# Two packed projections of the compression branch, each given its own duplicated weight piece

## The reference, cut to what matters

```python
(nq, nkc, nvc, nks, nvs, nkw, nvw, ngate, cq, ckv, kr, fq, fk, fv, ff) = jnp.split(h @ w_in, split_points, axis=-1)
tok_idx = jnp.arange(n_cmp)[:, None] * D_CMP + jnp.arange(L_CMP)[None, :]     # 15 windows of 32 tokens
def compress(kv, pe, w1, w2):
    blocks = kv[:, tok_idx] + pe[None, None, :, None, :]
    flat = blocks.transpose(0, 1, 3, 2, 4).reshape(B, n_cmp, G, L_CMP * DH)   # G = 2 groups, DH = 64
    return jax.nn.gelu(flat @ w1) @ w2
kc = compress(k_cmp, cmp_pe[0], cmp_w1[0], cmp_w2[0])
vc = compress(v_cmp, cmp_pe[1], cmp_w1[1], cmp_w2[1])
...
gates = jax.nn.sigmoid(h @ w_gate).reshape(B, S, 3, D_MODEL)
```

## Time and profile before

| | |
|---|---|
| median of 3 runs | 1681.83 us (1680.05 to 1681.88) |
| the profiled execution's own time | 1681.88 us |
| its span in the trace | 1680.1 us |
| PE busy | 1645.6 us, 98% |
| PEld (weight loads) busy | 1507.6 us, 90% |
| DVE, ACT, POOL busy | 62%, 43%, 32% |
| chain that ended last | PE 82%, DVE 11%, ACT 4% |
| granted TensorE clock | 0.998 of full speed |

### The profile page before, as it was taken

One profiled execution on the slowest core, in us unless ns is written; L12 is line 12 of the kernel. 1 busy time (PEld: TensorE's weight loads), 2 busy tenths in 40 slices (PEclk: granted clock), 3 DMA queues, 4 the chain that ended last, 5 costly groups with the idle time before them and its releaser, 6 DMA issues.

```text
span 1680.1 us, 34114 instructions
## 1 busy us (share of the span) xinstructions
PE 1645.6 (98%) x15064; PEld 1507.6 (90%) x15064; DVE 1033.9 (62%) x1661; ACT 714.2 (43%) x1124; POOL 539.6 (32%) x434
## 2 busy tenths in 40 slices
PE   9999999999999999999999999999999999999997
PEld 8888987899989889988888899999999899999996
DVE  5275376877774554776777877753346768643357
ACT  4444444544455544445444445432222555322223
POOL 0644613000307636321001304625542009154530
PEclk9999999999999999999999999999999999999999
DMA  9422355776546323456775544533223445332323
GB/s 353 155 101 76 129 213 204 262 280 256 184 161 234 127 76 118 155 217 243 283 281 196 176 169 146 189 107 121 102 102 130 151 149 204 111 125 101 127 77 113
DMA packets 44004, 281.46 MB, mean 168 GB/s; under 512 B 5144, under 2 KB 5272, under 8 KB 14416
## 3 DMA queue, kind: packets, MB, share of 16 engines
q1 hardware_dynamic: 42192, 270.13, 45.0%
q0 software_dynamic: 1664, 9.15, 1.4%
HBM read 278.20 MB, written 1.06 MB: 166 GB/s over the span
## 4 chain that ended last, share of the span: by engine, by line
PE 82%; DVE 11%; ACT 4%; issue 2%; DMA 0%; POOL 0%; POOLq 0%; SPq 0%; ACTq 0%; DVEq 0%
PE ps L537 79%; PE ps L545 3%; DVE part0l L1333 2%; DVE part1l L1333 2%; ACT part0h L2356 1%; ACT Xh L2356 1%; DVE rows L1757 1%; ACT part1h L2356 1%; DVE Xl L1348 1%; DVE Pr L1754 1%; ACT gates L2353 0%; DMA ring<-in_w 0%; DVE small L1364 0%; DVE sg L2020 0%; DVE x L1357 0%
## 5 line engine op out<-in xcount | busy, mean ns | idle before, releaser
L2356 ACT ACTIVATE part1h<-ring 128x1024 fp32r<-128x1024 f32 (+1 forms) x216 | 215.7, 1046 | 257.1 <-PE ps L537 245.6
L2356 ACT ACTIVATE part0h<-ring 128x1024 fp32r<-128x1024 f32 (+1 forms) x216 | 213.0, 1034 | 251.5 <-PE ps L537 241.6
L537 PE MATMUL ps<-Xh,part1h 128*128 128x256 f32 x1032 | 299.8, 291 | 6.7 <-DVE part1l L1333 2.5
L537 PE MATMUL ps<-Xh,part0h 128*128 128x256 f32 (+1 forms) x1016 | 294.4, 290 | 3.2 <-DVE Xl L1348 1.3
L537 PE MATMUL ps<-Xl,part1h 128*128 128x256 f32 x1032 | 292.6, 283 | 0.0
L537 PE MATMUL ps<-Xh,part1l 128*128 128x256 f32 x1032 | 292.3, 283 | 0.0
L537 PE MATMUL ps<-Xl,part0h 128*128 128x256 f32 (+1 forms) x1016 | 287.2, 283 | 0.0
L537 PE MATMUL ps<-Xh,part0l 128*128 128x256 f32 (+1 forms) x1016 | 287.0, 282 | 0.0
L1333 DVE TENSOR_TENSOR part1l<-ring,part1h 128x1024 fp32r<-128x1024 f32 (+1 forms) x148 | 187.9, 1309 | 58.1 <-ACT part1h L2356 57.7
L2858 POOL TENSOR_TENSOR part0l<-ring,part0h 128x512 fp32r<-128x512 f32 x136 | 173.5, 1309 | 154.8 <-ACT part0h L2356 154.8
L1333 DVE TENSOR_TENSOR part0l<-ring,part0h 128x1024 fp32r<-128x1024 f32 (+2 forms) x148 | 183.2, 1278 | 62.2 <-ACT part0h L2356 62.0
(11 more groups left out here) (413 smaller groups left out, 3275.6 us busy)
## 6 DMA issues: line engine op xcount, KB each, us to landing
ring<-in_w SPq DMA_DIRECT2D x211, 1024.0 KB, 4.9
hid<-in_ada SPq DMA_DIRECT2D x36, 512.0 KB, 5.8
hid<-in_w SPq DMA_DIRECT2D x6, 1024.0 KB, 10.7
rows<-in_lnrow POOLq DMA_DIRECT2D x6, 1024.0 KB, 9.6
fqk<-in_ada SPq DMA_DIRECT2D x6, 512.0 KB, 5.8
cq<-in_ada SPq DMA_DIRECT2D x6, 512.0 KB, 6.0
gates<-in_c SPq DMA_DIRECT2D x2, 1536.0 KB, 9.8
ring<-in_w SPq DMA_DIRECT2D x4, 512.0 KB, 5.8
```

The source lines that it names most:

```text
L537: return e.matmul(o, a, b, start=st, stop=sp)
L2356: return e.activation(o, a, ACT.Copy)
```

## The change

The piece `cmp` is replaced by two pieces, `cmpk` and `cmpv`, each a full 1 MB. Each holds its 128 columns twice: group 0, group 0, group 1, group 1, of 64 columns each. Half 0 of the new piece gives group 0 on both halves of the partitions, half 1 group 1. Both go through `gemm_half`, and `cmp_proj` becomes two copies for the keys and two for the values, each over both groups and within its own partitions. In the fills the four new halves take the slots n0 to n3; every gate half moves two places on, and the phase "m" takes ten halves in place of eight.

```diff
-FIRST = """misc fq fk fv cq0 cq1 nq0 nq1 kskw vsvw cmp g0_0 g0_1 g0_2 g0_3 g1_0 g1_1 g1_2
+FIRST = """misc fq fk fv cq0 cq1 nq0 nq1 kskw vsvw cmpk cmpv g0_0 g0_1 g0_2 g0_3 g1_0 g1_1 g1_2
...
-             "n": "cmp.0 mla0|cmp.1 mla1|g0_0.0 key1|g0_0.1 latents h0|g0_1.0 a0|g0_1.1 up h1|g0_2.0 a1|g0_2.1 turn kc|cs0 g0_3.0|cT0 g0_3.1|"
-                  "cs1 g1_0.0|cT1 g1_0.1|cv0 g1_1.0|cv1 g1_1.1|g1_2.0|g1_2.1|g1_3.0|g1_3.1",
-             "m": "g2_0.0 g2_0.1|g2_1.0 g2_1.1 OT0|g2_2.0 OT1|g2_2.1|OT3 g2_3.0|g2_3.1"}
+             "n": "cmpk.0 mla0|cmpk.1 mla1|cmpv.0 key1|cmpv.1 latents h0|g0_0.0 a0|g0_0.1 up h1|g0_1.0 a1|g0_1.1 turn kc|cs0 g0_2.0|cT0 g0_2.1|"
+                  "cs1 g0_3.0|cT1 g0_3.1|cv0 g1_0.0|cv1 g1_0.1|g1_1.0|g1_1.1|g1_2.0|g1_2.1",
+             "m": "g1_3.0 g1_3.1|g2_0.0 g2_0.1 OT0|g2_1.0 g2_1.1 OT1|g2_2.0 g2_2.1|OT3 g2_3.0|g2_3.1"}
...
-        elif name[0:4] == "cmp.":
-            m = int(name[4])
-            gemmT(l, ("cmpk", "cmpv")[m], "cmp", X, xkey(l), widths=(128,), col0=128 * m, frees=m == 1)
...
     def cmp_proj(l, s_):
-        t = bank(("cmpk", "cmpv")[s_], l)
+        b = v(bank(("cmpk", "cmpv")[s_], l)[:, :], g=2, n=256)
...
-        for g in range(2):
-            h = slice(64 * g, 64 * g + 64)
-            e.tensor_copy(M.dup[0:64, s_, g, :], t[h, 0:256]).then_inc(*V())
-            e.tensor_copy(M.dup[64:128, s_, g, 0:255], t[h, 1:256]).then_inc(*V("dup", s_, l))
+        e.tensor_copy(M.dup[0:64, s_, 0:2, :], b[0:64]).then_inc(*V())
+        e.tensor_copy(M.dup[64:128, s_, 0:2, 0:255], b[64:128, :, 1:256]).then_inc(*V("dup", s_, l))
...
-            if name[0:4] == "cmp.":
-                cmp_proj(l, int(name[4]))
+            if name in ("cmpk.1", "cmpv.1"):
+                cmp_proj(l, int(name == "cmpv.1"))
...
-        put(l, "cmp", cat(wi[:, nkc], wi[:, nvc]))
+        for key, c in (("cmpk", wi[:, nkc]), ("cmpv", wi[:, nvc])):
+            put(l, key, cat(c[:, 0:64], c[:, 0:64], c[:, 64:128], c[:, 64:128]))
```

More of the change, by code:

```diff
@@ L47, in piece_keys @@
     for l in range(L):
-        keys += [(l, k) for k in ("nq0", "nq1", "kskw", "fq", "fk", "cmp", "vsvw", "fv", "cq0", "cq1", "misc")]
+        keys += [(l, k) for k in ("nq0", "nq1", "kskw", "fq", "fk", "cmpk", "cmpv", "vsvw", "fv", "cq0", "cq1", "misc")]
         keys += [(l, f"g{b}_{j}") for b in range(3) for j in range(4)]
```

## The result

The changed kernel takes 1691.77 us (median of 4 runs, 1690.21 to 1692.54), the kernel before, run beside it, 1681.07 (4 runs, 1680.05 to 1681.88). The ratio is 1.0062, with an interval of 1.0048 to 1.0077: slower by 10.7 us, where 11.45 were forecast and 1693.3 for the time. Both times come in two groups about 1.5 us apart (36 times of the kernel before: 18 from 1679.93 to 1680.67, 18 from 1681.28 to 1682.31, none between), so a median of four can lie in either.

What follows compares the result with a forecast made beforehand. TensorE's stream, 98% busy, was taken to set the end. 1681.88 us + 11.45 for added matmuls, with 0 for copies, supply and gate shift, gave 1693.3 us; range 1690.5 to 1697.0.

Steps and rivals of the forecast that it cites:

- Part 1: TensorE in m2 and m3: 48 added matmuls per layer cost 5.73 us a layer, 11.45 us in both.
- The sum: Whole kernel: 1681.88 us plus 11.45 for added matmuls, all other terms 0, gives 1693.3 us, +0.68%.
- own range: Whole kernel: forecast within 1692.3 to 1694.5 us, from matmul bounds and 0.5 for execution differences; chance 0.84.
- waits are won: Rival: TensorE's stall in n7 goes altogether, 11.45 - 1.9 = 9.6 us added, 1691.4 us; chance 0.05.
- Part 2: VectorE's copies in n0 to n3: 0.69 us each, cost 0; covers 0.14 us, then 0.2 at n5.
- That rival: Stall on top: VectorE's delay in n3 to n5 (1695.7 us) or late supply in m (1699.3); chance 0.09.
- Part 3: Splitting and loading one more piece, in m: cost 0, with a cover of 1.5 us.
- Part 4: ScalarE's order in n7: the `kc` wait moves to its second product; gain 0, bound 1.9 us.
- The hidden case: Rival: added halves in m2 and m3 hide in TensorE's overlapping durations, 1680.0 us; chance 0.02.
- What would show it: Expected signs: n 98.5 us, m 37.2, m2 and m3 like m0, 8 copies of 0.69, waits about 2.2 a layer.

Runs made afterwards that it cites:

- e2: Kernel before, with each of the two halves of `cmp` computed twice (the same 96 matmuls, in n instead of m): 1690.67 us, ratio 1.0058.
- e3: Changed kernel, with the values' two copies in n3 done three times on VectorE: 1691.70 us, ratio 1.0063.
- e9: Changed kernel, with every second GpSimd subtraction doubled for `g2_0`, `g2_1` and `g2_2` (7.5 us a piece): 1694.43 us, one run.
- e7: Changed kernel, with GpSimd's subtractions for `g2_0`, `g2_1` and `g2_2` done twice (10 us a piece instead of 5): 1712.23 us, ratio 1.0184.
- e4: Kernel before, with ScalarE's gate activation first and the coming piece's two copies last in n7 and n9: 1677.90 us, ratio 0.9979.
- e5: Changed kernel, with the same ScalarE reordering in n7 and n9: 1687.73 us, ratio 1.0038 to the kernel before.
- e1: Changed kernel, with the four halves of `cmpk` and `cmpv` (n0 to n3) cut from 24 to 12 matmuls: 1693.59 us, ratio 1.0072.
- e8: Changed kernel, with the four halves of `g2_1` and `g2_2` (m2 and m3) cut from 24 to 12 matmuls: 1681.45 us, ratio 1.0002.
- e10: Changed kernel, with the values' pair of copies in n3 done five times on VectorE: 1697.08 us, one run.

## Why the prediction was right, step by step

- **Part 1, added matmuls: right.** 5.73 us a layer forecast, 5.76 found in m and 5.73 in e2's n. The row that carried it was the distance of starts inside a half. By the gap that the Trainium skill, "TensorE: Matmul & The Clock Gate", section "Back-to-back issue gap", gives for a matmul without its weight load, 109 ns for 256 columns, it would have been 10.5 us; the added matmuls have 119 to 120. That 10.5 lies nearer to the measured 10.7 is luck: it comes from the term of the next point, not from the distance of the starts.
- **The sum: its mechanism right, one term missing.** By the traces the two phases gained 11.35 us, and 11.2 to 11.3 came through to the end of layer 1's m. The stretch behind it gives back 1.2 to 1.4 us, so the change comes to about 10 us and not 11.45. The prediction took all that lies behind m to be as long as before.
- **The time: the forecast's own range was missed.** 1691.77 lies within 1690.5 to 1697.0 but under the "own range 1692.3 to 1694.5", 1.6 us below the forecast and 0.4 above the 1691.4 of the rival "waits are won". The time alone could not have told the two apart; the timeline of n7 does. Of the 1.6 us, 0.8 is the starting point: the sum set out from 1681.88, an execution of the longer group, and the kernel before had a median of 1681.07 beside the changed one. The 0.5 allowed for executions was too small for groups 1.5 us apart. (The bounds named give 1692.5 to 1694.6, not 1692.3 to 1694.5.)
- **Part 2, VectorE's copies: cost 0 was right, durations too (0.68 and 0.69), the covers wrong.** "So the covers are 1.52 - 1.38 = 0.14 us and then 0.2" failed: VectorE is idle for 0.52 us ahead of the MLP step in the changed kernel, and the scaling in n5 ends at 583.62 + 0.67 = 584.29, 0.63 ahead of scores at 584.92. The step treated VectorE's durations as fixed. Those of the MLP step are set by GpSimd's end in this slot, and e3 hid 2.8 us more. That rival deserved less than most of the 0.09.
- **Part 3, the supply: cost 0 right, cover too small.** 1.5 us were worked out, 2.0 and 2.7 read from the trace after, about 2 by e9. The price of a stall there was also too low, since the clock falls behind it (e7).
- **Part 4, ScalarE's order: right, in place and in size.** The wait went from `kc`'s first product to its second, 3.28 against 3.22 us from the gate's end. "Waits won" needs `fqk` ahead of the copies too. Where e4 and e5 do that, and n10 with it, 1.92 and 1.85 us a layer come out: about twice the bound that part 4 set from n7's `hid` waits alone (1.9 for both layers), since the 0.17 on `fqk` and n10's 0.6 go as well.
- **The hidden case: excluded.** e2 paid in full in n, where 14.7 us had no weight load, and the change paid in full in m, where 1.65 had none. The start times decide, not the uncovered part of the weight loads. By the Trainium skill, "Perfetto Trace Analysis", section "Identifying the Most-Contended Engine", weight-load busy time is, beside the share of peak arithmetic, the measure of TensorE's headroom; for the weight loads these runs do not bear that out. (That nothing but PE was above 62% left out their 90%.)
- **What would show it** held: n within 0.1, m at 37.23, m2 and m3 like m0, 8 copies of 0.69, waits of 2.2 us a layer (1.1, 0.6 and 0.5).

## What to carry to other kernels

Where an engine's stream sets the end, price what is added by the distance from one start to the next, not by shown durations or idle shares; but do not price what is taken out by the same number, because work in a tight place can be the cover of another engine, and a wait that is uncovered can cost clock as well (e1 against e8). A wait that goes away only counts when the next instruction's releaser has been followed too: here a change of order alone, with both releasers ahead of the long copies, was worth 1.9 us a layer and the shift alone nothing. Read the stretches behind the change before carrying a sum to the end. And where times come in groups, compare traces of the same group: the difference of two medians of four was off by up to a microsecond here.

## What the runs showed of the hardware

- VectorE operations on 30 columns took 1.20 to 1.23 us beside GpSimd's subtractions of 1.26 us and 0.18 to 0.19 without them. In n3 the last of them ended with GpSimd's piece, to within 0.05 us, both before and after the change.
- TensorE's granted clock fell from 1.00 to 0.50 for a few us near waits of 3.19 and 2.34 us (e7), 2.8, 1.9 and 1.5 (e1, layer 1 and twice layer 0), 2.5 (e10, layer 0) and 1.97 to 2.51 (the start, eight traces). It did not near waits of 1.34 (e7), 1.9 (e1, layer 1), 2.42 (e10, layer 1) and up to 2.00 at the start (six traces). So the length of the wait alone does not decide it, and what does stays open. In e7 it cost 3.1 us a layer on top of 6.9 of waits, and at the start of the kernel about 1.5 us, which fits the two groups of times.
- A copy of 64 partitions x 512 out of PSUM takes 0.68 us, as one of 128 x 512 does (0.69).
